# Moving the layer-1 ada products into the pool projection, and the dense chunk of a mixed step ahead of its transposes

## Chip, cores and metric

The kernel runs on one core of one Trainium2 chip. The metric is the device time of one execution in microseconds (us); lower is better. The profile is one execution taken by the hardware profiler on that core. Engines are PE (TensorE), DVE (VectorE), ACT (ScalarE), POOL (GpSimd) and SP (SyncE, which here only issues DMAs). DMAs are issued by SP, ACT and POOL in the order of their programs.

## What is computed

Two layers of a streaming encoder over 544 rows (512 prompt rows and 32 sample rows), model width 2048, all weights float32. Layer 0 is attention (8 heads of differential attention, 8 heads of latent attention), layer 1 is a pooling mixer. Both are modulated by a conditioning vector.

```python
cond = silu(c)
for i in range(2):
    mod = cond @ w_ada[i] + b_ada[i]
    shift, scale, gate = split(mod, 3)
    h = rmsnorm(x, g_norm[i]) * (1 + scale) + shift
    if i == 0:
        z = h @ w_in_att                       # q, k, v, latents, gate
        o = concat(diff_attention(...), latent_attention(...)) * silu(gate)
        y = o @ w_out_att
    else:
        u, g = split(h @ w_in_pool, 2)
        d = trailing_mean(u_ext, window 2/4/8/16) - u
        y = ((d @ w_grp) * scale_pool * silu(g)) @ w_out_pool
    x = x + gate * y
return rmsnorm(x, g_final), caches
```

The modulation `mod` is a product of a vector with a 2048 x 12288 matrix. Its last 16 column tiles are the gate of layer 1. They are first used at the very end, when layer 1's output is added to x.

## The kernel before

Activations lie transposed: features on the 128 partitions, the 544 rows along the free axis. A weight tile is 128 output features by 2048 inputs (1 MB). A dense product splits weights and activations into a high and a low part and adds three products (hi·hi, hi·lo, lo·hi); so one weight tile is 16 k-steps of 6 matmuls, 96 matmuls of 272 columns, into one of two accumulators of two PSUM banks. `split` (DVE, L1562 and L1563) makes the two parts of a whole tile from `w_raw`; the buffer of the parts has two slots, so the split of tile g waits until tile g-2 is multiplied.

The stages, in order, with the times of the profile:

- to 1014 us: modulation, input projection, latent attention.
- 1014 to 1217 us, the differential attention, L1041 on. It is a hand-written order of 39 mixed steps w. In a step PE makes the scores of unit w (`d_scores`), now and then the transposes of a head's values, the products of a finished head with its values (`d_values`), the transposes of unit w-3 (`d_turn`), and a chunk of 2 or 3 of the 8 k-steps of a dense half tile (`latent_half`, the latent heads' half of the output projection; three steps make one half tile). DVE makes the row maximum of unit w, ACT the two exponentials (L1381), DVE the normalised scores (L1862), ACT and DVE the two parts of the transposed scores (L1403 and L1883). ACT may write the exponentials of unit w only when unit w-3 is transposed (`df_tr`), as three buffers rotate. `evict_half` (ACT, L1353) empties the dense half tile from PSUM after every third step, and PE's next half tile waits for it; the result goes over POOL (an addition to x) and `store_half` to memory.
- 1217 to 1282 us: the end of the attention, and the loads of the next stage.
- 1282 to 1440 us, here called the O2 loop: the differential heads' half of the output projection, 16 half tiles (g = 81 to 96) of 48 matmuls. For each, ACT evicts with the gate (L1467), ACT makes the upper part of a later tile's weights (`half_hi`, L1339), DVE adds to x (`update`, L1923) and makes the lower part (`half_lo`, L1819), ACT squares, POOL adds the squares. Beside each half tile DVE makes one ada product: `ada_tile` (L1600) multiplies a 1 MB tile `w_adr` with the two conditioning rows `cond_b` and sums, 128 x 2048 twice, then copies two numbers into `mod`. The tiles of `w_adr` (two buffers) are loaded by ACT (`load_ada`, L1235), which waits for the product that frees the buffer.
- 1440 to 1477 us: the norm of layer 1 (`row_scale`, `affine1`, `make_h1`).
- 1477 to 1852 us, the pool projection (PIN): 16 turns t of two tiles, the u tile A(t) and the gate tile B(t). DVE in a turn: split of B(t), wait for ACT's copy of u, windows and differences, split of A(t+1), wait for the store of the differences. SP loads the tiles of `w_in_pool` into the two slots of `w_raw` as the splits free them.
- to the end: group maps, output projection, final norm.

The SP program around the change issues, in order: `sel_row`, `cond_b` (2 MB), two `w_adr` tiles (1 MB each), two half tiles of `w_out` (0.5 MB each), x back from memory.

## Time and profile before

| what | value |
|---|---|
| median of 3 runs | 2124.44 us (2120.06 to 2126.26) |
| profiled execution, its own time | 2125.24 us |
| its span in the trace | 2123.5 us |
| PE busy | 1876.0 us (88%) |
| DVE busy | 1272.3 us (60%) |
| ACT busy | 454.6 us (21%) |
| POOL busy | 198.6 us (9%) |
| mean DMA rate | 149 GB/s |
| chain that ended last, PE's share | 70% |
| chain that ended last, DVE's share | 14% (L1600: 4%) |

The shares are of the whole span. The digits of PE in 40 slices are 9 nearly everywhere from slice 7 on; they fall to 8 and 7 between slices 19 and 27 (1000 to 1470 us), which is where the change works. The clock granted to PE falls there too, to 7 and 8 tenths.

### The profile page before, as it was taken

Reading aid. Unit: us, or ns where it says so; the run is one execution under the profiler, and the core shown is the slowest. Engines: PE = TensorE matmul, PEld = TensorE weight load, DVE = VectorE, ACT = ScalarE, POOL = GpSimd, SP = SyncE. Lnnn points to the kernel's source line nnn. Section 1 sums busy time; section 2 is a strip of 40 time slices with the busy share of each in tenths; the row PEclk is TensorE's granted clock in tenths of the full one; section 3 lists DMA queues with packets and bytes.
Section 4 is the critical chain, followed back from the end, with each engine's and each line's share of the span. In section 5 each row is a group of like instructions: output and inputs, shape, how many; then the busy total and the mean of one; then the engine's idle time right before and its main releaser. Section 6 shows DMA issues by size and latency. Waiting matters only on the chain.

```text
span 2123.5 us, 32736 instructions
## 1 busy us (share of the span) xinstructions
PE 1876.0 (88%) x13182; PEld 1724.6 (81%) x13182; DVE 1272.3 (60%) x1598; ACT 454.6 (21%) x959; POOL 198.6 (9%) x117
## 2 busy tenths in 40 slices
PE   4539999999999969998888887776999999999995
PEld 0109999999999957767777767765999999999995
DVE  4898766767867644551556547788333444483444
ACT  1241000000011013231555433223111111131111
POOL 3760000000600000000000011110000000001110
PEclk8779999999999999997889988886999999999997
DMA  9565554556545331214333264441333233462222
GB/s 392 207 239 187 199 204 184 201 196 236 209 184 207 131 114 54 67 67 119 102 115 117 89 235 165 168 157 51 109 115 108 100 107 123 150 203 97 81 79 84
DMA packets 86104, 316.04 MB, mean 149 GB/s; under 512 B 12184, under 2 KB 20552, under 8 KB 60448
## 3 DMA queue, kind: packets, MB, share of 16 engines
q1 hardware_dynamic: 62192, 223.02, 29.2%
q10 hardware_dynamic: 23216, 91.16, 12.1%
q0 software_dynamic: 640, 1.10, 0.1%
q8 instruction: 36, 0.59, 0.1%
q14 instruction: 20, 0.16, 0.0%
HBM read 282.56 MB, written 32.69 MB: 148 GB/s over the span
## 4 chain that ended last, share of the span: by engine, by line
PE 70%; DVE 14%; ACT 5%; DMA 3%; issue 3%; POOL 2%; ACTq 1%; SPq 0%; DVEq 0%; POOLq 0%
PE banks L712 70%; DVE banks L1600 4%; POOL ssq L670 2%; DMA w_more<-in_w_ada_pe 1%; ACT pxd L1381 1%; DMA w_raw<-in_w_out 1%; DVE std L1835 1%; ACT w_hi L1339 1%; DVE h_lo L394 1%; DMA d_raw<-pool_d_scratch 1%; ACT stage L1467 1%; DVE rstd L1542 1%; DVE x L2029 0%; DVE w_lo L1563 0%; DMA sgd<-gate_scratch 0%
## 5 line engine op out<-in xcount | busy, mean ns | idle before, releaser
L712 PE MATMUL banks<-h_hi,w_hi 128*128 128x272 f32 x3968 | 836.7, 297 | 76.6 <-DVE w_lo L1819 33.3
L712 PE MATMUL banks<-h_lo,w_hi 128*128 128x272 f32 x3712 | 783.2, 293 | 0.0
L712 PE MATMUL banks<-h_hi,w_lo 128*128 128x272 f32 x3456 | 728.3, 293 | 0.0
L712 PEld LDWEIGHTS banks<-h_hi,w_hi 128*128 128x128 f32 x3968 | 639.9, 195 | 89.8 <-issue 66.2
L712 PEld LDWEIGHTS banks<-h_lo,w_hi 128*128 128x128 f32 x3712 | 601.2, 194 | 0.0
L712 PEld LDWEIGHTS banks<-h_hi,w_lo 128*128 128x128 f32 x3456 | 552.7, 193 | 0.0
L1600 DVE CUSTOM_DVE_ANT_0 banks<-w_adr,cond_b 128x2048 f32<-128x2048 f32 x160 | 402.3, 2514 | 18.6 <-DMA w_adr<-in_w_ada_dve 11.4
L1562 DVE CAST w_hi<-w_raw 128x2048 fp32r<-128x2048 f32 x101 | 125.6, 1244 | 215.4 <-PE banks L712 210.9
L1563 DVE TENSOR_TENSOR w_lo<-w_raw,w_hi 128x2048 fp32r<-128x2048 f32 x101 | 249.2, 2467 | 3.5
L1245 ACT ACTIVATE stage<-banks 128x544 f32<-128x544 f32 x48 | 30.2, 629 | 515.3 <-PE banks L712 515.3
L695 POOL TENSOR_TENSOR ssq<-ssq,stage 128x544 f32<-128x544 f32 x32 | 49.7, 1552 | 790.5 <-ACT stage L1168 790.5
L1923 DVE TENSOR_TENSOR x<-x,stage 128x544 f32 (+1 forms) x32 | 23.2, 725 | 138.0 <-ACT stage L1467 138.0
L1965 DVE TENSOR_TENSOR w<-u_ext 128x573 f32<-128x573 f32 x16 | 12.1, 756 | 138.8 <-ACT u_ext L1490 138.8
L1467 ACT ACTIVATE stage<-banks,mod 128x272 f32<-128x272 f32 (+2 forms) x96 | 32.6, 410 | 250.3 <-PE banks L712 165.7
L712 PE MATMUL banks<-w_more,cond_t 128*2 128x512 f32 x80 | 43.4, 700 | 36.9 <-DMA w_more<-in_w_ada_pe 23.2
L712 PEld LDWEIGHTS banks<-w_more,cond_t 128*2 128x2 f32 x80 | 7.0, 93 | 72.0 <-issue 44.3
L712 PE MATMUL banks<-w_raw,cond_t 128*2 128x512 f32 x48 | 29.1, 764 | 34.5 <-DMA w_raw<-in_w_ada_pe 34.5
L712 PEld LDWEIGHTS banks<-w_raw,cond_t 128*2 128x2 f32 x48 | 4.3, 98 | 57.6 <-DMA w_raw<-in_w_ada_pe 32.0
L712 PE MATMUL banks<-cq,wq 128*128 128x272 f32 x128 | 34.3, 425 | 14.2 <-DVE cq L1698 9.0
L1381 ACT ACTIVATE pxd<-banks,std 128x128 f32<-128x128 f32 (+3 forms) x64 | 33.2, 524 | 60.6 <-DVE std L1836 38.5
L701 POOL TENSOR_TENSOR cos_t<-cos_t,kpe 128x544 f32<-128x544 f32 x8 | 10.8, 1353 | 372.2 <-ACT act_tmp L1357 372.2
L712 PEld LDWEIGHTS banks<-cq,wq 128*128 128x128 f32 x128 | 25.7, 206 | 21.5 <-issue 16.0
(296 smaller groups left out, 1735.8 us busy)
## 6 DMA issues: line engine op xcount, KB each, us to landing
w_adr<-in_w_ada_dve ACTq DMA_DIRECT2D x60, 1024.0 KB, 4.9
w_raw<-in_w_z SPq DMA_DIRECT2D x32, 1024.0 KB, 6.2
w_raw<-in_w_pin SPq DMA_DIRECT2D x32, 1024.0 KB, 4.8
w_adr<-in_w_ada_dve SPq DMA_DIRECT2D x20, 1024.0 KB, 4.9
w_raw<-in_w_gate SPq DMA_DIRECT2D x16, 1024.0 KB, 6.6
w_raw<-in_w_out SPq DMA_DIRECT2D x32, 512.0 KB, 3.8
w_raw<-in_w_pout SPq DMA_DIRECT2D x16, 1024.0 KB, 4.9
w_more<-in_w_ada_pe SPq DMA_DIRECT2D x10, 1024.0 KB, 7.3
```

The costliest lines, as they stand in the source:

```text
L394: ins = eng.scalar_tensor_tensor(out=h_lo[:, k, r], in0=x[:, k, r], scalar=mod[:, c, k:k + 1], in1=h_hi[:, k, r].bitcast(F32), op0=ALU.add ...
L670: pool.tensor_tensor(ssq[:], ssq[:], (stage[:, 0], rstd[:])[k % 2], ALU.add).then_inc(sq_added, 1)
L695: pool.tensor_tensor(ssq[:], ssq[:], stage[:, s], ALU.add).then_inc(sq_added, 1)
L712: return pe.matmul(out, lhsT, rhs, start=start, stop=stop)
L1245: act.activation(rows(stage[:, s]), acc[slot], func).then_inc(acc_free[slot], 1)
L1339: act.activation(half_slots(g)[0], w_raw[:, g % 2, 0:D // 2], ACT.Copy).then_inc(w_upper, 1)
L1381: ins = act.activation(pxd[:, w % 3, e, 0:n], PS[:, 2 * (w % 2) + e, 0:n], ACT.Exp, bias=std[:, w, 2 + e:3 + e], scale=DIFF_SCALE, accum_o ...
L1467: ins = act.activation(stage[:, s, r], PS[:, 2 * slot + bank, cols], ACT.Identity, scale=mod[:, c, bass.ds(2 * t + (gate_tile + s), 1)])
L1562: vchain(dve, dve.tensor_copy(w_hi[:, slot], w_raw[:, slot]))
L1563: dve.tensor_tensor(w_lo[:, slot], w_raw[:, slot], w_hi[:, slot].bitcast(F32), ALU.subtract).then_inc(split_ready, 1)
L1600: ins = dve.tensor_tensor_reduce(ada_junk, w_adr[:, slot], cond_b[:, c, :], 1.0, 0.0, ALU.mult, ALU.add, ada_acc[:, c:c + 1])
L1923: dve.tensor_tensor(at(x, t2 + k), at(x, t2 + k), stage[:, slot], ALU.add).then_inc(x_new, 1)
```

## The change

- The 16 ada products of layer 1's gate leave the O2 loop. They are made in the first 8 turns of the pool projection, two in each: one after the split of B(t), one after the split of A(t+1).
- There they have one buffer, `w_adr[:, 1]`, as the first one's place is used by `u_ext`, `w2` and `w4`; a filler `under_ada` moves `d_st` and `fix` behind `w_adr` and `cond_b`. Their 16 loads are issued by SP, in turn t behind those of A(t) and B(t), each waiting until the product before it is done. The two loads ahead of the O2 loop and ACT's loads in it are gone.
- The Silu of `cond_b` on ACT moves from before the O2 loop to behind `affine1`, and DVE's wait for it to before the first turn of the pool projection.
- In a mixed step PE makes the dense chunk after the values' transposes and before `d_values` and `d_turn`; before, it came last.
- ACT's `evict_half` moves from the end of every third step to the start of the step after it, `store_half` to the end of the step with w % 3 == 1. The small ACT instruction that told POOL of the eviction (`x1_ev`) is gone; POOL waits for `acc_free`.

```diff
+        sb("under_ada", [P, 6466], scope=pin_stack)
...
@@ SP
-            for s in range(2):
-                load_ada(s, w_ada_dve[ADA_P0 + ADA_P1 + s])
...
-            with sp.Fori(0, KT) as t:
+            with sp.Fori(0, KT // 2) as t:
                 for s in range(2):
                     load_w(tile_of(wp2, s, t), (G_PIN + s) % 2, 2 * t + G_PIN - G_KPE + s)
+                for s in range(2):
+                    sp.wait_ge(adr_used, 2 * t + (ADA_P0 + ADA_P1 + s))
+                    sp.dma_start(w_adr[:, 1], tile_of(wd2, s, t + (ADA_P0 + ADA_P1) // 2)).then_inc(adr_in[s], 16)
+            with sp.Fori(KT // 2, KT) as t:
+                for s in range(2):
+                    load_w(tile_of(wp2, s, t), (G_PIN + s) % 2, 2 * t + G_PIN - G_KPE + s)
+            sp.wait_ge(adr_used, ADA_P0 + ADA_P1 + KT)
@@ POOL
-                pool.wait_ge(x1_ev, n + 1)
+                pool.wait_ge(acc_free[(G_OUT + n) % 2], turn_of(G_OUT + n) + 1)
@@ PE, a mixed step
+                if w < 3 * IN_STEPS:
+                    latent_half(w // 3, chunk_of[w % 3])
                 for h in range(HEADS):
                     if w == d_last(h) + DLAG + 1:
                         d_values(h)
                 if DLAG <= w < D_UNITS + DLAG:
                     d_turn(w - DLAG)
-                if w < 3 * IN_STEPS:
-                    latent_half(w // 3, chunk_of[w % 3])
@@ ACT, evict_half
-                act.wait_ge(acc_free[g % 2], turn_of(g) + 1)
-                act.activation(act_tmp[0:1, 0:1], act_tmp[0:1, 0:1], ACT.Copy).then_inc(x1_ev, 1)
@@ ACT, a mixed step
-            for w in range(D_UNITS + DLAG + 2):
+            for w in range(D_UNITS + DLAG + 1):
+                if w % 3 == 0 and w:
+                    evict_half(w // 3 - 1)
...
-                if w < 3 * IN_STEPS and w % 3 == 2:
-                    if w // 3:
-                        store_half(w // 3 - 1)
-                    evict_half(w // 3)
+                if w % 3 == 1 and w > 3:
+                    store_half(w // 3 - 1)
...
-            act.wait_ge(condb_in, 32)
-            act.activation(cond_b[:], cond_b[:], ACT.Silu).then_inc(condb_ready, 1)
...
-                gated(t, G_O2, 1, 2 * KT, ADA_P0 + ADA_P1, True)
+                gated(t, G_O2, 1, 2 * KT, halves=True)
...
             affine1()
+            act.wait_ge(condb_in, 32)
+            act.activation(cond_b[:], cond_b[:], ACT.Silu).then_inc(condb_ready, 1)
@@ DVE, O2 loop
-            dve.wait_ge(condb_ready, 2)
...
-                    ada_tile(ADA_P0 + ADA_P1 + s, 2 * t, t)
                     update(G_O2 + s, 2 * t, t, 1, s, s)
                     half_lo(G_O2 + s + 2, 2 * t, t)
...
-                ada_tile(ADA_P0 + ADA_P1 + k, 0, 0)
@@ DVE, pool projection
+            dve.wait_ge(condb_ready, 2)
             for grp, w in enumerate(WIN):
                 with dve.Fori(4 * grp, 4 * grp + 4) as t:
...
                     split(G_PIN + 1, dve_t2, t)
+                    if grp < 2:
+                        ada_tile(ADA_P0 + ADA_P1, dve_t2, t, 1)
                     dve.wait_ge(acc_free[us], t + turn_of(G_PIN + 2))
...
                     split(G_PIN + 2, dve_t2, t)
+                    if grp < 2:
+                        ada_tile(ADA_P0 + ADA_P1 + 1, dve_t2, t, 1)
                     dve.wait_ge(d_stored, 16 * t + 16)
+                if grp == 1:
+                    add_bias(ADA_PE + ADA_P0 + ADA_P1, ADA_T)
```

## Rows read from the trace of the kernel before

**Rows 1.** Stretch, us, busy of PE, PEld, DVE, ACT, POOL; PE's clock, DMA share, GB/s.

```profile
1014.00:1213.00 199.00, 168.78 (x1228) 147.56 (x1227) 115.86 (x260) 108.49 (x297) 16.22 (x12) 0.89 0.34 108
...
1282.00:1440.00 158.00, 112.03 (x716) 108.35 (x715) 126.58 (x117) 41.70 (x81) 26.43 (x17) 0.83 0.47 162
...
1477.00:1574.00 97.00, 96.75 (x772) 96.76 (x773) 36.80 (x49) 16.13 (x26) 0.00 (x0) 1.00 0.34 121
```

**Rows 2.** The chain that ended last: start us, us, what, count.

```profile
1242.18 14.67 DMA w_raw<-in_w_out
...
1438.32 2.19 PE banks L712 x4
...
1477.25 373.11 PE banks L712 x2976
```

**Rows 3.** PE's waits, 1213 to 1480 us: waited for, total us, times, longest.

```profile
PE banks L712 <- DVE w_lo L1819: 33.3, 14, 4.6
```

**Rows 4.** Timeline of DVE, one half tile and the end of the O2 loop.

```profile
1291.36 3.43 DVE L1600 CUSTOM_DVE_ANT_0 banks<-w_adr,cond_b 128x2048 f32<-128x2048 f32 x1
...
1299.23 0.73 DVE L1923 TENSOR_TENSOR x<-x,stage 128x544 f32 x1 [1.67 <-ACT stage L1467]
1300.05 1.22 DVE L1819 TENSOR_TENSOR w_lo<-w_raw,w_hi 128x1024 fp32r<-128x1024 f32 x1
1301.19 3.44 DVE L1600 CUSTOM_DVE_ANT_0 banks<-w_adr,cond_b 128x2048 f32<-128x2048 f32 x1
...
1435.44 0.72 DVE L1923 TENSOR_TENSOR x<-x,stage 128x544 f32<-128x544 f32 x1
```

**Rows 5.** Timeline of PE between half tiles 82 and 83.

```profile
1286.60 0.41 PE L712 MATMUL banks<-h_hi,w_lo 128*128 128x272 f32 x2
1291.58 0.81 PE L712 MATMUL banks<-h_hi,w_hi 128*128 128x272 f32 x2 [4.57 <-DVE w_lo L1819]
```

**Rows 6.** DMA issues of three moments: engine, count, KB, us to landing.

```profile
cond_b<-in_cB SPq DMA_DIRECT2D x1, 2048.0 KB, 9.8
...
w_adr<-in_w_ada_dve SPq DMA_DIRECT2D x1, 1024.0 KB, 4.8
w_raw<-in_w_z SPq DMA_DIRECT2D x1, 1024.0 KB, 6.6
...
w_raw<-in_w_out SPq DMA_DIRECT2D x2, 512.0 KB, 6.3
```

**Rows 7.** Timeline of ACT and DVE: the Silu, and the entry of the pool projection.

```profile
1278.78 3.62 ACT L1456 ACTIVATE cond_b<-cond_b 128x4096 f32<-128x4096 f32 x1
...
1472.01 1.28 ACT L1486 ACT_TABLE_LOAD   x1
...
1473.64 1.23 DVE L1562 CAST w_hi<-w_raw 128x2048 fp32r<-128x2048 f32 x1 [0.32 <-DVE h_lo L1581]
1474.90 2.29 DVE L1563 TENSOR_TENSOR w_lo<-w_raw,w_hi 128x2048 fp32r<-128x2048 f32 x1
```

**Rows 8.** Timeline of DVE: an ada product beside the input projection, POOL idle.

```profile
184.61 2.29 DVE L1600 CUSTOM_DVE_ANT_0 banks<-w_adr,cond_b 128x2048 f32<-128x2048 f32 x1
...
189.50 0.17 DVE L1606 COPY mod<-ada_acc 128x2 f32 x1
```

**Rows 9.** PE's waits in the mixed steps, 1014 to 1213 us.

```profile
PE banks L1012 <- DVE pxd L1862: 11.8, 4, 3.0
PE banks L1009 <- ACT od L1411: 5.3, 3, 1.8
```

**Rows 10.** Timeline of mixed steps 5 to 8: PE and ACT.

```profile
1044.33 1.00 ACT L1353 ACTIVATE rstd<-banks,mod 128x272 f32<-128x272 f32 x3
...
1042.97 1.11 PE L1012 MATMUL banks<-id_t,pxd 128*128 128x128 f32 x4 [2.96 <-DVE pxd L1862]
1045.48 0.79 PE L712 MATMUL banks<-h_hi,w_hi 128*128 128x272 f32 x2 [1.39 <-ACT rstd L1353]
...
1052.70 0.37 ACT L1381 ACTIVATE pxd<-banks,std 128x128 f32<-128x128 f32 x1 [2.63 <-PE banks L1012]
```

More of the change, by code:

```diff
@@ L361, in program @@
         x_new = sem("x_new")
-        w_upper = sem("w_upper"); x1_ev = sem("x1_ev"); x1_added = sem("x1_added")
+        w_upper = sem("w_upper"); x1_added = sem("x1_added")
         x1_in = [sem(f"x1_in{s}") for s in range(2)]
@@ L1593, in make_h1, with ada_tile @@
                 dve.wait_ge(h_ready, 2 * KT + 2)
-            def ada_tile(a, t2, t):
+            def ada_tile(a, t2, t, buf=None):
                 slot = a % 2
@@ L1599, in ada_tile @@
                 for c in range(2):
-                    ins = dve.tensor_tensor_reduce(ada_junk, w_adr[:, slot], cond_b[:, c, :], 1.0, 0.0, ALU.mult, ALU.add,
+                    ins = dve.tensor_tensor_reduce(ada_junk, w_adr[:, slot if buf is None else buf], cond_b[:, c, :], 1.0, 0.0, ALU.mult, ALU.add,
                                                    ada_acc[:, c:c + 1])
@@ L1926, in _ @@
             half_lo(G_O2 + 1)
-            dve.wait_ge(condb_ready, 2)
             dve.wait_ge(x_in, 32)
             with dve.Fori(0, KT // 2 - 2) as t:
-                dv.loop(t, 4)
                 for s in range(2):
-                    ada_tile(ADA_P0 + ADA_P1 + s, 2 * t, t)
                     update(G_O2 + s, 2 * t, t, 1, s, s)
                     half_lo(G_O2 + s + 2, 2 * t, t)
-            dv.end(KT // 2 - 2)
             dve.wait_ge(x_rest_in, 16)
             for k in range(KT - 4, KT):
-                ada_tile(ADA_P0 + ADA_P1 + k, 0, 0)
                 update(G_O2 + k, 0, 0, 1, k, k % 2)
@@ L1943, in _ @@
                     split(G_PIN)
-            add_bias(ADA_PE + ADA_P0 + ADA_P1, ADA_T)
             dve.memset(lam_in[:, 0, 0:1], 0.0).then_inc(pad_free, 1)
@@ L1955, in _ @@
                     t0 = t - 4 * grp
-                    dv.loop(t0, 2 + grp + 1 + 1 + 1)
+                    dv.loop(t0, 2 + grp + 1 + 1 + 1 + (4 if grp < 2 else 0))
                     dve_t2 = 2 * t
                     split(G_PIN + 1, dve_t2, t)
+                    if grp < 2:
+                        ada_tile(ADA_P0 + ADA_P1, dve_t2, t, 1)
                     dve.wait_ge(acc_free[us], t + turn_of(G_PIN + 2))
```

## Prediction

> **What bounds the kernel now.** I read the busy time by stretch first, then the chain that ended last, then PE's waits and the timelines of the two loops. PE is the bound of the whole, but not of every stage [rows 1]: in the pool projection it is busy 96.75 of 97 us at full clock (2.4 GHz) while DVE works 36.8 us; in the O2 loop it is busy 112 of 158 us at a mean clock of 0.83, and DVE 127 of 158. PE there waits 33.3 us in 14 waits for the lower part of the weights [rows 3]. One half tile shows why: DVE's round from one ada product to the next is 1301.19 - 1291.36 = 9.83 us, of which `update` and `half_lo` are 0.73 and 1.22 and the product the most [rows 4]. So the O2 loop is bound by DVE, through the products, which nobody needs there. The reader should see one engine short in one stage and long in the next.
>
> A full tile costs PE 373.11 us / 31 = 12.04 us at full clock: 2976 matmuls are 31 tiles of 96 [rows 2]. A half tile is then 6.02 us, a turn of the pool projection 24.07 us.
>
> **Part 1: the end of the attention.** SP no longer issues two 1 MB loads between `cond_b` and the first half tile of `w_out`. That tile's landing is on the chain with 14.67 us [rows 2]. A second 1 MB transfer issued 0.4 us behind a first lands 6.6 + 0.4 - 4.8 = 2.2 us after it; 2 MB alone take 9.8 [rows 6]. The wait falls to between 9.8 (the row of 2 MB, as if half a megabyte cost nothing more) and 14.67 - 4.4 = 10.3; with what was issued in between I take 5.0 us gained. All that follows up to half tile 82 moves with it. The Silu of `cond_b` (1.28 us table, 3.62 us [rows 7]) stood on ACT between half tile 82's weights and the first eviction; PE was multiplying 82 meanwhile, so it costs nothing by itself once the products are gone.
>
> **Part 2: the O2 loop.** Half tile 82 ended at 1286.9 [rows 5]; now 1281.9. Half tile 83 needs its weights: SP issues them behind the last part of x, after `store_half(15)`, which also moves by 5; they land 6.3 us after issue [rows 6], near 1280.4, and the two parts (about 1.0 on ACT, 1.2 on DVE) are there at 1282.7, 0.8 us late. What is late next in the loop? Per half tile DVE now has 0.73 + 1.22 us, ACT the eviction and `half_hi` (about 1 us each) and a square of 0.7, and the chain from the end of g to the weights of g+2 is about 3.5 us, 4.7 if POOL holds DVE up once; PE works 6.02 us on g+1 meanwhile. So PE is the bound, and its clock stays at the upper level as in the pool projection [rows 1]. Fourteen half tiles: 1282.7 + 84.3 = 1367.0. From the last matmul to the row sums: eviction and semaphore 1.2 us, then as now from `update` (1435.44) to the row sums (1438.32) 2.9 us [rows 2, 4]: 1371.1. The gain up to that point is 1438.3 - 1371.1 = 67.2 us, part 1's 5.0 included. Bounds: 8 us less if a half tile takes 6.6 us, nothing more.
>
> **Part 3: the entry of the pool projection.** The norm is unchanged, 33 us on DVE. Then DVE waits for the Silu before the split of B(0). ACT ends `affine1` at 1472.0, where its next table load starts [rows 7]; table 1.28 and Silu 3.62 end at 1476.95, and DVE began the split at 1473.64 [rows 7]. PE waits for this split (it ended at 1477.2, where PE's long piece begins [rows 2]). Cost 3.3 us, all on the path.
>
> **Part 4: the turns with products.** A product with its copy takes 189.67 - 184.61 = 5.06 us beside a busy PE and an idle POOL [rows 8]; in the O2 loop the first half took 3.43 instead of 2.29 [rows 4] with POOL at work, and POOL is idle in the pool projection [rows 1]. Two in a turn are 10.1 us on a DVE busy 36.8 in four turns, 9.2 in each: 19.3 of 24.07 us. By busy time they are hidden. By order they are not, because one buffer and SP's order tie the loads to the products. Per turn, in order, the end of one releasing the next: the split of A(t+1), 3.5 us [rows 7]; the product behind it, 5.06; only then SP issues the next `w_adr` tile, 4.8 + 0.1 us to landing less 0.2 as the semaphore comes before the copy, 4.7 [rows 6]; the product of that tile, 5.06; only then SP issues the other `w_adr` tile and, behind it on the same queue, A(t+2), which lands 0.4 + 6.6 us later less 0.2, 6.85 [rows 6]; then its split. The sum is 3.5 + 5.06 + 4.7 + 5.06 + 6.85 + 0.2 of handovers = 25.4 us against PE's 24.07. The loop is PE's no longer, by 1.3 us a turn. In the first turn, counted from the end of B(0)'s split: product 5.06, A(1) lands at 11.9, is split at 15.5, and PE, done with B(0) at 12.03, waits 3.4 us. The eighth such split ends at 15.5 + 7 x 25.4 = 193.3; PE would have been there at 12.03 + 7 x 24.07 = 180.5. Cost 12.8 us, with part 3 16.1. Queued behind DVE's waits are the windows and splits; behind SP's wait for `adr_used` the tiles of `w_in_pool`, which is the whole cost. ACT waits for `d_ready` before the gate's Silu, and PE needs that accumulator only a tile later. From turn 8 on everything is as before.
>
> Bounds: if the loop hides under PE, 3.3 + 3.4 = 6.7 us; if A lands only when all three queued megabytes are in (2 MB alone take 9.8 [rows 6]; 2.4 more a turn), 15.5 + 2.4 + 7 x 27.8 - 180.5 + 3.3 = 35.3. I take 16, as the row with two megabytes in a queue is the nearest.
>
> The Trainium skill, DMA: Bandwidth & Descriptors, Rules for kernel authors, advises to issue a DMA early, compute, and wait for it late. The new loop does the reverse for half of its loads. The same page, Bandwidth, gives 6.15 us for 1 MB where this trace has 4.8 [rows 6]; an estimate with the page's figure adds 1.35 us to each of the two landings in a turn and would make the turn 28.1 us. The trace's duration is the one I use.
>
> **Part 5: the mixed steps.** PE waits for the normalised scores 11.8 us in four waits and for the eviction of `od` 5.3 us [rows 9]; a chunk put in front (18 matmuls, 2.3 us) covers part of these. But the order speaks against it twice. Step 6 shows the first: PE waited 2.96 us for the scores, transposed, then 1.39 us for the eviction on ACT, 1044.33 + 1.0 [rows 10]. The chunk needs that eviction, so in front of the transposes it waits for both; ACT's place for it is the same as before, as nothing stood between the end of step 5 and the start of step 6. The second: ACT's exponentials of unit w wait until w-3 is transposed. This bound already in step 7, 2.63 us idle [rows 10]; now the transposes come one chunk, 2.3 us, later in every step. ACT and DVE pass work to one another, so part of this reaches the next step. Followed through steps 3 to 15 with the durations of the timeline, the chunk of step 6 comes 1.5 us later and that of step 15 2.8: 1.3 us per nine steps, 5.4 for four such groups. The last `store_half` comes one step earlier, so SP reaches the load of `sgd` sooner, about 1.3 us. I take +4 us. Bounds: the two waits covered whole, -17; one chunk lost in each of the 12 handovers of a half tile, +28; for the range I use -12 and +12. The dropped ACT instructions and POOL's other semaphore (0.2 us, 16 times) lie beside PE's work; nothing.
>
> **The sum**, against the profiled execution's own 2125.24 us: -67.2 + 3.3 + 12.8 + 4.0 = -47.1, so 2078.1. That execution stands 0.8 us above the median of the three runs, which changes nothing; I give 2078.
>
> **The rivals.**
> - The loop with products hides (A lands sooner, the handovers are shorter): the cost of parts 3 and 4 is 6.7 instead of 16.1, 2069. For it: the margin is 1.3 us in 25.4. Against: the row of the landing is direct. Chance 0.15.
> - The mixed steps gain: the chunk covers the waits of rows 9, -12 instead of +4, 2062. For it: 17 us of waits stand right behind the scores. Against: rows 10. Chance 0.15.
> - Late landing: A(t+1) lands with the third tile of its queue; 35.3 instead of 16.1, 2097. For it: 9.8 us for 2 MB. Beside this stands a rule of the Trainium skill, DMA: Bandwidth & Descriptors, Queues, rings and completion order: completion is not first in, first out for one issuing engine. Chance 0.12.
> - Something else bounds the O2 loop: PE's half tile becomes 7.2 us, because POOL's additions stretch DVE's `half_lo` or the 0.5 MB loads come late: 14 x 1.2 = 17 us less gained, 2095. Against: 3.5 us of work in a 6.02 us window. Chance 0.08.
> - Slower: the single buffer of `w_adr`. If both landings of the chain in part 4 take 3.8 us more, near 8.6 and 10.6 (2 MB took 9.8), the turn is 33 us: 7 x 9 + 10.5 = 73 against 63 gained, 2135. It decides from 32 us a turn. Nothing but the first loads behind `cond_b` comes near that. Chance 0.04.
> - The change doesn't do what it says: a wait left in place keeps ACT's eviction in the O2 loop behind something else, and the loop stays at 9.8 us a tile while the products cost as well: about 2132. I find no such wait. Chance 0.01.
> - My forecast: 0.45.
>
> **The numbers.** The likeliest case gives 2078. The range that holds 8 in 10 takes the two faster rivals and the late landing in: 2060 to 2099. 0.3% (6.4 us) is about what a measurement tells from no change; faster than that are all cases but the last two, 0.94, slower 0.05, same 0.01.
>
> **What would show it.** PE's waits for `half_lo` in the O2 loop near zero, the loop 84 to 88 us for 14 half tiles, clock near 1.0. DVE's wait for `cond_b` before the first turn. In the turns with products: pieces of PE separated by 1 to 2 us, waits for DVE's w_lo L1563 and behind them w_raw, period 25.4; DVE waiting for w_adr about 1 us twice a turn or less; SP's waits for the product. In the mixed steps: no wait for pxd, a longer one for the eviction (up to 7 us in step 6), ACT waiting for PE's transposes far more than now. I am wrong if the period is under 24.2 or over 27, if a half tile is over 6.4 us, or if the mixed steps move by more than 8 us.

## The result: 0.5% faster, where 2.2% was forecast

The changed kernel takes 2112.28 us (median of 6 runs, 2108.93 to 2112.97), the kernel before 2123.07 beside it (6 runs). The ratio is 0.9947, with a 95% interval of 0.9933 to 0.996. It is faster by about 11 us. The forecast was 47 us less, and the range ended at 2060 and 2099: the time lies above it.

The profiled execution of the changed kernel took 2112.39 us, with a span of 2110.6 (before 2125.24 and 2123.5), so the two traces differ by 12.9 us and can be compared stage by stage. Line numbers are up by 4 to 6: TensorE's products are L718 (were L712), the transposes L1018, the evictions of the mixed steps L1359, the exponentials L1387, DVE's product L1604, the split L1566 and L1567, `half_lo` L1823.

The chain that ended last, of the changed kernel (start us, us, what, count), to be read beside [rows 2]; the row at 1404.36 is the row sums of layer 1's norm:

```profile
1273.96 11.37 DMA w_raw<-in_w_out
...
1315.95 84.46 PE banks L718 x672
...
1404.36 2.19 PE banks L718 x4
...
1438.06 1.28 ACT L1484
1439.35 3.63 ACT cond_b L1484
1443.35 1.24 DVE w_hi L1566
...
1452.59 6.72 DMA w_raw<-in_w_pin
...
1467.80 4.87 DMA w_adr<-in_w_ada_dve
...
1478.47 6.69 DMA w_raw<-in_w_pin
```

The reader sees the O2 loop as one piece of PE (672 matmuls, 14 half tiles), then the Silu in front of B(0)'s split, then landings of `w_raw` in every turn, where before one piece of 373.11 us stood. The loop itself went as forecast. But it starts late: `w_out` is asked for at 1273.96, and at 1242.18 before. These 31.8 us lie in the mixed steps, ahead of all the rest. The same stretch of both traces shows it (first before, then after; stretch, us, busy of PE, PEld, DVE, ACT, POOL; PE's clock, DMA share, GB/s):

```profile
1014.00:1243.00 229.00, 197.50 (x1420) 170.19 (x1418) 131.72 (x278) 120.65 (x320) 19.25 (x14) 0.91 0.36 115
```

```profile
1014.00:1243.00 229.00, 185.22 (x1237) 162.49 (x1238) 113.04 (x261) 106.01 (x284) 16.19 (x12) 0.80 0.28 94
```

PE does fewer matmuls in the same time, is idle for 12 us more, and its mean clock is 0.80 instead of 0.91. The waits of that stretch after the change (waited for, us in total, times, longest), first ACT's, then PE's; before, the exponentials waited 21.7 us in 7 for the transposes, and PE 4.6 and 2.8 for the evictions:

```profile
ACT pxd L1387 <- PE banks L1018: 74.7, 15, 10.4
ACT pxd L1387 <- DVE std L1840: 28.8, 17, 2.7
```

```profile
PE banks L718 <- ACT rstd L1359: 17.8, 4, 7.0
PE banks L718 <- ACT kpe L1359: 17.0, 5, 7.0
```

PE's wait for `pxd` [rows 9] is gone, as forecast. In its place PE waits 34.8 us for evictions, where it was 7.4.

Cutting the two profiles at the same events gives the whole difference:

| stretch, from which event to which | before | after | change | forecast |
|---|---|---|---|---|
| start to the issue of `w_out` (mixed steps) | 1242.18 | 1273.96 | +31.8 | +4.0 |
| landing of `w_out` | 14.67 | 11.37 | -3.3 | -5.0 |
| landing to the row sums (O2 loop) | 181.5 | 119.0 | -62.4 | -62.2 |
| row sums to the end of B(0)'s split (Silu) | 38.9 | 42.5 | +3.6 | +3.3 |
| from there to the eighth split of an A (before: PE's own time for it, 180.5, worked out in the prediction) | 180.5 | 197.9 | +17.4 | +12.8 |

The sum is -12.9, which is the difference of the spans; what follows the last row takes the same time in both within 0.2 us. One term of five is wrong by 28 us, another by 4.6, and the landing by 1.7.

### The profile page after: what moved, and what is told of

It reads as the page before. It is cut to its first block, busy times and chain, and to the rows that moved or that the text cites. A ratio compares the mean times of both kernels' runs of the same rounds, so it can differ in the third digit from the quotient of the medians.

```text
span 2110.6 us, 32711 instructions
## 1 busy us (share of the span) xinstructions
PE 1874.6 (89%) x13182; PEld 1722.4 (82%) x13182; DVE 1253.6 (59%) x1598; ACT 411.3 (19%) x912; POOL 198.4 (9%) x117
## 4 chain that ended last, share of the span: by engine, by line
PE 65%; DVE 13%; DMA 8%; ACT 6%; issue 5%; POOL 2%; SPq 1%; DVEq 0%; ACTq 0%; POOLq 0%
PE banks L718 65%; DVE banks L1604 3%; DMA w_raw<-in_w_pin 3%; POOL ssq L676 2%; DMA w_adr<-in_w_ada_dve 2%; DMA w_more<-in_w_ada_pe 1%; ACT pxd L1387 1%; DMA d_raw<-pool_d_scratch 1%; DMA w_raw<-in_w_out 1%; DVE w_hi L1566 1%; DVE std L1839 1%; DVE h_lo L395 1%; DVE w_hi L1823 1%; DVE rstd L1546 1%; DVE x L2034 0%
## 5 line engine op out<-in xcount | busy, mean ns | idle before, releaser
L718 PE MATMUL banks<-h_hi,w_hi 128*128 128x272 f32 x3968 | 832.7, 295 | 86.6 <-DVE w_lo L1567 29.6
L718 PE MATMUL banks<-h_lo,w_hi 128*128 128x272 f32 x3712 | 778.1, 292 | 0.0
L718 PE MATMUL banks<-h_hi,w_lo 128*128 128x272 f32 x3456 | 721.0, 290 | 0.0
L718 PEld LDWEIGHTS banks<-h_hi,w_hi 128*128 128x128 f32 x3968 | 634.6, 194 | 98.9 <-issue 72.6
L718 PEld LDWEIGHTS banks<-h_lo,w_hi 128*128 128x128 f32 x3712 | 596.3, 193 | 0.0
L718 PEld LDWEIGHTS banks<-h_hi,w_lo 128*128 128x128 f32 x3456 | 545.7, 191 | 0.0
L1604 DVE CUSTOM_DVE_ANT_0 banks<-w_adr,cond_b 128x2048 f32<-128x2048 f32 x160 | 386.2, 2414 | 19.2 <-DMA w_adr<-in_w_ada_dve 16.0
L1566 DVE CAST w_hi<-w_raw 128x2048 fp32r<-128x2048 f32 x101 | 125.6, 1244 | 220.1 <-PE banks L718 169.4
L1567 DVE TENSOR_TENSOR w_lo<-w_raw,w_hi 128x2048 fp32r<-128x2048 f32 x101 | 249.2, 2467 | 3.5
L718 PE MATMUL banks<-w_more,cond_t 128*2 128x512 f32 x80 | 43.7, 704 | 39.0 <-DMA w_more<-in_w_ada_pe 22.8
L718 PEld LDWEIGHTS banks<-w_more,cond_t 128*2 128x2 f32 x80 | 7.0, 94 | 74.3 <-issue 47.1
L1887 DVE TENSOR_TENSOR ptd_lo<-banks,ptd_hi 128x128 fp32r<-128x128 f32 (+3 forms) x32 | 15.7, 492 | 81.4 <-ACT ptd_hi L1409 81.4
L718 PE MATMUL banks<-w_raw,cond_t 128*2 128x512 f32 x48 | 29.0, 760 | 32.6 <-DMA w_raw<-in_w_ada_pe 32.6
L1387 ACT ACTIVATE pxd<-banks,std 128x128 f32<-128x128 f32 (+3 forms) x64 | 33.2, 524 | 103.5 <-PE banks L1018 74.7
L718 PEld LDWEIGHTS banks<-w_raw,cond_t 128*2 128x2 f32 x48 | 4.3, 98 | 55.6 <-DMA w_raw<-in_w_ada_pe 30.2
L718 PE MATMUL banks<-cq,wq 128*128 128x272 f32 x128 | 34.3, 425 | 14.3 <-DVE cq L1702 9.0
```

What stands on the lines that cost most here:

```text
L718: return pe.matmul(out, lhsT, rhs, start=start, stop=stop)
L1387: ins = act.activation(pxd[:, w % 3, e, 0:n], PS[:, 2 * (w % 2) + e, 0:n], ACT.Exp, bias=std[:, w, 2 + e:3 + e], scale=DIFF_SCALE, accum_o ...
L1566: vchain(dve, dve.tensor_copy(w_hi[:, slot], w_raw[:, slot]))
L1567: dve.tensor_tensor(w_lo[:, slot], w_raw[:, slot], w_hi[:, slot].bitcast(F32), ALU.subtract).then_inc(split_ready, 1)
L1604: ins = dve.tensor_tensor_reduce(ada_junk, w_adr[:, slot if buf is None else buf], cond_b[:, c, :], 1.0, 0.0, ALU.mult, ALU.add, ada_acc[: ...
```

## Experiments: is it the mixed steps, and which part of them?

Every ratio below is against the kernel before, measured beside the run. The runs were made in four groups, in which its medians were 2126.40, 2127.52, 2124.97 and 2126.65 us; beside the changed kernel it was 2123.07. So differences between medians of different groups are uncertain by some 4 us.

**One or both parts undone.** The first run keeps the move of the products and takes the steps back; the others add the steps, or one of their two edits, to the kernel before.

```diff
                 if DLAG <= w < D_UNITS + DLAG:
                     d_turn(w - DLAG)
+                if w < 3 * IN_STEPS:
+                    latent_half(w // 3, chunk_of[w % 3])
```

(Cut to TensorE's order of before; in the first run `x1_ev` and the evictions and stores at the end of the third step come back too.)

> The changed kernel with its mixed steps put back as they were (TensorE's dense chunk last, evictions at the end of the third step of a half tile, the x1_ev operation); the products stay moved. Theory A, the loss sits in the mixed steps and is worth what their stretch shows (58.3 us per nine steps against some 50 to 51.5 before, four and a half turns of nine, about 31 us): 2112 - 31 = 2081 us, so 0.98 of before. Rival B, the mixed steps cost the 4 us that was forecast and the rest of the gain went elsewhere in the program: 2112 - 4 = 2108 us. Between 2095 and 2100 neither is right alone.

Measured: 2080.28 us, ratio 0.979 (0.9764 to 0.9816). The steps cost 32.0 us, theory A. Rival B is out. With them taken back, the kernel is near the forecast, in part by luck: without the 4 us that the forecast gave to the steps it would have been 2074, and the 6 us above that are the 4.6 and 1.7 us by which part 4 and the landing were off.

The next three start from the kernel before: both edits, the order alone, the evictions alone. The edit on ScalarE, cut to its main lines (the old places of the eviction and the store go, and with them `x1_ev`), is

```diff
-            for w in range(D_UNITS + DLAG + 2):
+            for w in range(D_UNITS + DLAG + 1):
+                if w % 3 == 0 and w:
+                    evict_half(w // 3 - 1)
...
+                if w % 3 == 1 and w > 3:
+                    store_half(w // 3 - 1)
```

> The kernel before with the mixed steps of the changed one (dense chunk ahead of the transposes, evictions at the start of the next half tile's first step, no x1_ev operation) and nothing else. Theory A (the steps alone cost about 31 us): 2123 + 31 = 2154 us, ratio 1.015. Rival B (4 us): 2127 us, ratio 1.002. Rival C, the steps are slow only because the products no longer stand elsewhere, which would make the two parts not add up: within 0.3% of before, 2117 to 2129.

Measured: 2157.93 us, ratio 1.0161 (1.0132 to 1.019), 31.5 us above before: the two parts of the change add up, and the steps' loss does not depend on the products.

> The kernel before with one edit: TensorE does the dense chunk ahead of the transposes; ScalarE's evictions stay at the end of the third step. Theory A1, the order on TensorE is all of the loss: 2150 to 2158 us, the same as with both edits. Rival A2, the loss comes from the evictions that stand behind the next turn's start: about 2123, within 0.3% of before. Rival A3, each needs the other: with evictions at the end of the third step and the chunk early, the next half tile's chunks find their banks free earlier and the time falls below before, to 2105 to 2117 us.

Measured: 2157.91 us, ratio 1.0156 (1.013 to 1.0183). TensorE's order is all of the loss (A1).

> The kernel before with the other edit alone: ScalarE evicts a half tile at the start of the next half tile's first step, stores in its second, and GpSimd waits for the eviction itself; TensorE's chunk stays last. Theory A1 (TensorE's order is the loss): 2120 to 2126 us, no change. Rival A2 (the place of the evictions is the loss): 2145 to 2158 us. Rival A3 (they hold only together): 2120 to 2126 too, so this run parts A2 from the others and the run with the chunk alone parts A1 from A3.

Measured: 2125.29 us, ratio 0.9997 (0.9984 to 1.001). The evictions' place and the dropped operation are worth nothing, as the prediction said.

**The mechanism.** Two places of every nine steps hold the long waits; waits of 2.95 and 2.5 us at two others complete the 74.7 us. The first is step 12, where the sample values stand. Timeline of the changed kernel, PE and then ACT (start us, us, engine, line, operation, count, in brackets the idle time before it):

```profile
1081.70 1.91 PE L718 MATMUL banks<-ptds,vcs 128*128 128x32 f32 x8
...
1086.52 0.82 PE L718 MATMUL banks<-h_hi,w_hi 128*128 128x272 f32 x2
...
1090.60 0.27 PE L1018 MATMUL banks<-id_t,pxd 128*128 128x128 f32 x1
```

```profile
1079.55 1.02 ACT L1359 ACTIVATE rstd<-banks,mod 128x272 f32<-128x272 f32 x3
1090.97 0.69 ACT L1387 ACTIVATE pxd<-banks,std 128x512 f32<-128x512 f32 x1 [10.39 <-PE banks L1018]
```

ACT has evicted by 1080.6, and its next exponentials need a buffer that one transpose of 0.27 us sets free. In front of that transpose PE now has scores, sample values and the chunk, 10.5 us of work. The clock was at its lower level, 1.2 GHz, all through: eight sample products took 1.91 us, scores and sample values together 6.5 us, and the chunk 4.1 us. In the kernel before, the clock was at its upper level when the scores and sample values came (3.9 us), and this step's chunk stood behind the transpose. But that chunk ran at the lower level there too, and took 4.0 us, from 1079.64 to 1083.60:

```profile
1076.88 1.08 PE L712 MATMUL banks<-ptds,vcs 128*128 128x32 f32 x8
...
1079.64 0.75 PE L712 MATMUL banks<-h_hi,w_hi 128*128 128x272 f32 x2
...
1083.60 0.50 PE L712 MATMUL banks<-kd_hi,qd_hi 64*128 64x512 f32 x2
```

So of the 6.6 us by which the work in front of the transpose grew, 4.1 are the chunk at its own price and 2.5 the lower clock on the rest.

The second place is step 15, three steps on:

```profile
1105.79 0.79 PE L718 MATMUL banks<-h_hi,w_hi 128*128 128x272 f32 x2 [6.97 <-ACT kpe L1359]
...
1110.01 1.01 PE L1018 MATMUL banks<-id_t,pxd 128*128 128x128 f32 x4
```

```profile
1104.64 1.01 ACT L1359 ACTIVATE kpe<-banks,mod 128x272 f32<-128x272 f32 x3
1111.12 0.47 ACT L1387 ACTIVATE pxd<-banks,std 128x256 f32<-128x256 f32 x1 [5.47 <-PE banks L1018]
```

PE waits 6.97 us for an eviction (1.39 before, at 1097.13). ACT then waits for the transposes behind the chunk. The chunk takes 4.2 us (mean clock 0.51 from 1105 to 1111); in the kernel before it took 3.8 (mean clock 0.60 from 1097.13 to 1100.92). One waits for the other in turn, where before PE's chunk ran beside ACT's exponentials.

**Waiting or slower work.** ACT's sample exponentials mark the period. Between the first and the last of them lie 27 steps, with the same matmuls in every kernel (columns as in the result's stretches; first before, then after):

```profile
1058.34:1207.70 149.36, 126.41 (x929) 110.58 (x929) 84.58 (x197) 79.04 (x221) 12.14 (x9) 0.91 0.34 109
```

```profile
1062.73:1236.37 173.64, 141.22 (x928) 123.73 (x927) 82.65 (x197) 76.90 (x212) 12.13 (x9) 0.79 0.28 93
```

The stretch grew by 24.3 us. PE is idle 9.5 us more (32.4 against 23.0), and busy 14.8 us more with the same work, at a mean clock of 0.79 instead of 0.91. This is an account and no experiment: at the upper level part of the 14.8 us could have turned into waits. The runs that follow are best read in the same way:

| run | start of the first marker | the 27 steps | PE busy in them | PE idle |
|---|---|---|---|---|
| before | 1058.3 | 149.4 | 126.4 | 23.0 |
| changed kernel | 1062.7 | 173.6 | 141.2 | 32.4 |
| every first chunk behind | 1061.4 | 158.1 | 132.3 | 25.9 |
| first chunk of 3, 12, 21, 30 behind | 1058.1 | 172.1 | 136.8 | 35.3 |
| first chunk of 6, 15, 24, 33 behind | 1061.8 | 171.7 | 138.9 | 32.8 |
| four buffers | 1055.1 | 153.1 | 129.1 | 24.0 |
| wait filled | 1056.7 | 172.5 | 149.1, filler included | 23.4 |

**Which chunk.** Three runs move the chunk back behind the transposes in some steps: in 0, 3, 6, ... (below); with `w % 9 == 3`, which has the steps with sample values 12, 21 and 30 (and step 3, which has none); and with `w % 9 == 6`, those behind the wait of 6.97 us.

```diff
-                if w < 3 * IN_STEPS:
+                if w < 3 * IN_STEPS and w % 3:
                     latent_half(w // 3, chunk_of[w % 3])
...
+                if w < 3 * IN_STEPS and w % 3 == 0:
+                    latent_half(w // 3, chunk_of[0])
```

> The changed kernel, but the first dense chunk of each half tile (steps 0, 3, 6, ...) goes back behind the step's values and transposes; the other two stay ahead of them. In the trace of the changed kernel every long wait of TensorE (6.97 us, in one first chunk of three) and every long wait of an exponential (10.39 us behind the sample values, 5.47 us) lies at a first chunk. Theory C, the loss comes from these: the chunk that itself waits for an eviction holds back the transposes that ScalarE needs before the next one. Then most of the 31 us comes back: 2082 to 2092 us. Rival D, each chunk ahead costs its own 2.4 to 4 us in front of a transpose, whichever it is: only a third comes back, 2098 to 2106 us.

Measured: 2088.53 us, ratio 0.9819 (0.9786 to 0.9853). some 24 of the 32 us come back with one chunk of three: theory C. (The four times spread from 2083.37 to 2093.17, and the trace is of the longest.)

> The changed kernel with the chunk back behind the transposes in the steps with sample values alone (3, 12, 21, 30). Theory K, these steps start it: sample values (5 us at the low clock) and the chunk (4.3 us) both stand before one short transpose, the exponentials wait 10.39 us, and everything on ScalarE, the eviction for which TensorE waits 6.97 us later too, is late by that. Then this alone brings back 15 to 24 us: 2088 to 2097 us. Rival L, the two places are separate costs: 4 to 10 us come back, 2102 to 2108 us.

Measured: 2108.76 us, ratio 0.9928 (0.99 to 0.9955): 3.5 us back by the medians, which is not clear of the noise (the changed kernel's interval, 0.9933 to 0.996, overlaps), a little less than rival L had, and far from theory K. ACT's longest wait falls from 10.4 to 6.1 us, but the sum stays:

```profile
ACT pxd L1389 <- PE banks L1018: 74.0, 18, 6.1
```

> The changed kernel with the chunk back behind the transposes in steps 6, 15, 24 and 33 alone, where TensorE waits 6.97 us for the eviction and then does the chunk at the low clock while the exponentials wait 5.47 us. Theory K (the steps with sample values start it): the transposes no longer wait for the eviction here, which brings back the 5.47 us of the exponentials in four places at most, less what moves to the next wait: 5 to 14 us, 2098 to 2107 us, less than the other run. Theory M, this is the place that starts it: 15 us or more, 2088 to 2097 us.

Measured: 2102.81 us, ratio 0.9893 (0.9867 to 0.9919); 9.5 us back by the medians, 4.2 by the spans of the traces. The number is in theory K's range, but K wanted less here than in the run before, and that one took K away; M's 15 us are not reached. K was argued from the two timelines above, and the table does not bear it: by the traces, of what the run with 3, 12, 21 and 30 gained, 4.6 us lie ahead of the first marker, where step 3 has no sample values, and only 1.6 in the 27 steps.

Neither place carries the loss alone: 3.5 and 9.5 are 13 us together (1.6 and 2.0 in the 27 steps), and all first chunks at once give 24 (15.5). Two explanations are left. The run with every first chunk also moves those of steps 0, 9, 18, 27 and 36, which neither of the two others does; at step 9 PE waits 1.38 us for the eviction, and the exponentials at 1068.06 wait 2.95 us for the transposes behind it. Or a wait that goes at one place comes back at the next, as long as another first chunk still stands in front. No run moves the third group alone, or any two of the three, so this stays open.

**The buffers.** The exponentials of step w overwrite what step w-3 left, so they need the transposes that PE does in step w itself. A fourth buffer moves that one step back.

```diff
-        pxd = sb("pxd", [P, 3, 2, NP], scope=dif)
+        pxd = sb("pxd", [P, 4, 2, NP], scope=dif)
...
-                        if w >= 3 and w % 9 != 2:
-                            act.wait_ge(df_tr, w - 2)
+                        if w >= 4 and w % 9 != 3:
+                            act.wait_ge(df_tr, w - 3)
```

> The changed kernel with four buffers for the exponentials instead of three, so that the exponentials of a step wait for the transposes of one step earlier (the tile vrs moves elsewhere to make room; all the work is kept). Theory E, the chain that costs the time runs from an eviction on ScalarE to TensorE's chunk, from there to the transposes behind it, and from these to the next exponentials: the 74.7 us of exponentials waiting for transposes fall below 30 and at least 20 us come back, 2080 to 2092 us. Rival F, TensorE waits for the evictions whatever the exponentials do, and the exponentials only wait because TensorE is late: no more than 6 us come back, 2106 to 2112 us.

Measured: 2086.9 us, ratio 0.9822 (0.9795 to 0.9848): 25 us come back, theory E. (The trace is of the fastest of the four, 2080.28 us.) The waits of ACT and PE in the same stretch are

```profile
ACT pxd L1387 <- DVE std L1840: 45.8, 32, 2.7
```

```profile
PE banks L718 <- ACT rstd L1359: 14.4, 4, 6.2
PE banks L718 <- ACT kpe L1359: 13.3, 5, 6.1
```

The exponentials wait for no transpose any more. PE's waits for evictions fall only from 34.8 to 27.7 us. They seem to have a cause of their own: ACT evicts when it has done a whole step, and the chunk now asks for that early. That they are the part of the loss that stays is argued.

**The clock.** In steps 6, 15, 24 and 33, 36 additional matmuls each fill PE's wait; their result is overwritten.

```diff
+                pe.wait_ge(df_exp, w)
+                for k in range(count):
+                    small(PS[:, 2 * ((w + 1) % 2), 0:240], w_hi[:, 0, 0:P], h_hi[:, HEADS, 0:240], True, True)
```

> The changed kernel with 36 additional matmuls of 240 columns in steps 6, 15, 24 and 33, between the scores and the first dense chunk, where TensorE waits 6.97 us for the eviction; their result is overwritten by the next scores. They wait for the exponentials of the step before (1101.04 in the trace, where the wait runs from 1098.82 to 1105.79) and last 3.5 to 4 us at the full clock, so they take no time from the chunk. They part the wait from the clock: the chunk and transposes behind the wait take 5.2 us now and 3.2 at the full clock. Theory G, the clock's fall behind that wait costs about 2 us in each of four places and brings more waits: 2098 to 2106 us. Rival H, the low clock there is covered by other waits, or the filler runs at the low clock itself and delays the chunk: 2110 to 2122 us.

Measured: 2107.76 us, ratio 0.9924 (0.9896 to 0.9953), 4.5 us back by the medians. That lies between the two theories (G ended at 2106, H began at 2110), and the interval overlaps the changed kernel's. Step 15 of that run; the first row is the 36 additional matmuls and the first two of the chunk:

```profile
1095.18 6.18 PE L718 MATMUL banks<-h_hi,w_hi 128*128 128x240 f32 x38 [2.27 <-ACT pxd L1395]
1101.19 0.41 PE L718 MATMUL banks<-h_lo,w_hi 128*128 128x272 f32 x2
...
1103.20 0.60 PE L1018 MATMUL banks<-id_t,pxd 128*128 128x128 f32 x4
1103.72 0.33 PE L718 MATMUL banks<-kd_hi,qd_hi 64*128 64x128 f32 x2
```

```profile
1098.73 1.01 ACT L1367 ACTIVATE kpe<-banks,mod 128x272 f32<-128x272 f32 x3
...
1103.89 0.47 ACT L1395 ACTIVATE pxd<-banks,std 128x256 f32<-128x256 f32 x1 [4.15 <-PE banks L1018]
```

Chunk and transposes run at the upper level (1.00 from 1101 to 1106), the four transposes in 0.60 us instead of 1.01, and the exponentials wait 4.15 us here instead of 5.47. All in all they still wait 73.4 us for transposes. But the filler was not free: it ran largely at the lower level itself (mean clock 0.71 from 1095.18 to 1100.98), took 5.7 us where 3.5 to 4 had been expected, and ended 1.1 us after the eviction (1099.74) for which the chunk had waited; in the last of the four places it was 3.5 us. So the run shows that the clock behind these waits is worth something, not how much: 4.5 us is what was left after the filler's own cost. By the traces the first marker comes 6.0 us earlier, and the 27 steps are only 1.1 us shorter. The low clock at the sample values was not filled at all.

## Experiments: the turns with products and the Silu

These start from the first run (steps as before, 2080.28 us).

```diff
...
+            with sp.Fori(0, KT // 2 - 1) as t:
+                load_w(tile_of(wp2, 1, t), (G_PIN + 1) % 2, 2 * t + G_PIN - G_KPE + 1)
+                load_w(tile_of(wp2, 0, t + 1), G_PIN % 2, 2 * t + G_PIN - G_KPE + 2)
+                sp.wait_ge(adr_used, 2 * t + (ADA_P0 + ADA_P1 + 1))
...
+                sp.wait_ge(adr_used, 2 * t + (ADA_P0 + ADA_P1 + 2))
```

> The changed kernel with its mixed steps as before and another order of SyncE's loads in the eight turns with products: the second and the next first tile of the input projection are issued ahead of the two waits for products, so each load of w_raw goes out when its buffer is free and not when a product is done. Theory I, the 21 us that these turns cost are this order: a load of w_raw stands behind a wait for a product, and DVE's products alone fit in the turn of 24.07 us, as the eight turns without them have it. The turns with products fall from 25.94 to about 24.1 us and the first by some 3 us: 2062 to 2067 us. Rival J, the products themselves fill DVE or the channels past 24 us: at most 5 us come back, 2075 to 2080 us.

Measured: 2085.7 us, ratio 0.9811 (0.978 to 0.9841): no gain, and 5.4 us above the same kernel without the new order, above rival J's range too. J's reason was not shown either: DVE was not full. A turn takes 27.2 us (1484.85 to 1512.06) instead of 25.97. SP's and DVE's timeline, SP's first:

```profile
1483.98 0.33 SPq L636 DMA_DIRECT2D w_adr<-in_w_ada_dve  x1
1484.85 0.92 SPq L470 DMA_DIRECT2D w_raw<-in_w_pin  x2
```

```profile
1491.89 1.23 DVE L1577 CAST w_hi<-w_raw 128x2048 fp32r<-128x2048 f32 x1 [7.76 <-DMA w_raw<-in_w_pin]
```

Both `w_raw` loads still stood behind the wait for the second product of the turn before. My order had only moved that wait. The next run issues each load in the order in which DVE lets its buffer go:

```diff
...
+            with sp.Fori(0, KT // 2 - 1) as t:
+                load_w(tile_of(wp2, 1, t + 1), (G_PIN + 1) % 2, 2 * t + G_PIN - G_KPE + 3)
+                sp.wait_ge(adr_used, 2 * t + (ADA_P0 + ADA_P1 + 1))
+                sp.dma_start(w_adr[:, 1], tile_of(wd2, 1, t + (ADA_P0 + ADA_P1) // 2)).then_inc(adr_in[1], 16)
+                load_w(tile_of(wp2, 0, t + 2), G_PIN % 2, 2 * t + G_PIN - G_KPE + 4)
+                sp.wait_ge(adr_used, 2 * t + (ADA_P0 + ADA_P1 + 2))
+                sp.dma_start(w_adr[:, 1], tile_of(wd2, 0, t + ((ADA_P0 + ADA_P1) // 2 + 1))).then_inc(adr_in[0], 16)
```

> The changed kernel with mixed steps as before and a third order of SyncE's loads in the turns with products: each load is issued in the order in which DVE lets go of its buffer (second w_raw tile after its split, w_adr after its product, first w_raw tile, w_adr). In the run with the loads ahead the order was wrong: both w_raw loads still left together behind a product (1484.85, right after w_adr at 1483.98) and DVE then stood 7.76 us for the first. Theory I', the cost of the turns with products is this order: no w_raw load stands behind a product, a turn is 24.1 us, and about 14 us of the turns' cost come back: 2063 to 2068 us. Rival J, DVE's products fill the turn by themselves: 2076 to 2082 us, as without the new order.

Measured: 2063.34 us, ratio 0.9709 (0.9688 to 0.9729), 16.9 us below the same kernel without the new order, theory I'. The chain has the input projection as one piece again, and PE is busy all through the turns with products, with DVE at 160.8 of 205 us:

```profile
1414.74 205.36 PE banks L727 x1619
```

```profile
1415.00:1620.00 205.00, 205.00 (x1620) 205.00 (x1621) 160.82 (x194) 12.73 (x40) 0.00 (x0) 0.99 0.55 188
```

So the products hide fully under PE, and SP's order was the cause of the 17.4 us of the result's table, within 0.5 us. The Trainium skill, DMA: Bandwidth & Descriptors, Rules for kernel authors, asks for early issue and a late wait; this pair (2080.28 and 2063.34 us) bears it out for loads that one engine issues in order.

```diff
             root(1)
-            affine1()
             act.wait_ge(condb_in, 32)
             act.activation(cond_b[:], cond_b[:], ACT.Silu).then_inc(condb_ready, 1)
+            affine1()
```

> The kernel of the loads in turn, with the Silu of cond_b on ScalarE ahead of affine1 instead of behind it, where ScalarE waits for the row sums' root and the fold. If the 3.6 us that Silu stands in the chain (1439.35, 3.63 us, of the changed kernel) is a matter of its place, 3 to 5 us below the kernel with the loads in turn; if ScalarE's work behind it only waits elsewhere or the table is loaded twice more, within 1 us of it.

Measured: 2057.66 us, ratio 0.9686 (0.9668 to 0.9703), 5.7 us less by the medians. By the traces, from the row sums to the end of B(0)'s split, it is 3.7. ACT's row shows where the Silu went, beside DVE's reciprocal:

```profile
1377.70 3.62 ACT L1494 ACTIVATE cond_b<-cond_b 128x4096 f32<-128x4096 f32 x1
```

The last two add the fourth buffer (the diff above), and then TensorE's order of the changed kernel with the evictions left where they were.

> The last one with four buffers for the exponentials and the chunk last, as before. In the steps before the change, exponentials wait 21.7 us for transposes in seven places and 38.5 us for DVE's maxima. If the seven waits are on the path: 5 to 12 us below the kernel with three buffers; if the next thing (DVE's maxima, the transposes waiting for DVE's pxd) takes their place: within 3 us of it.

Measured: 2057.71 us, ratio 0.9687 (0.9666 to 0.9708): nothing. With the chunk last, the fourth buffer frees exponentials that then wait for something else: no wait for transposes is left, but 52.7 us for DVE's maxima (39.6 with three buffers). PE's wait for `pxd` is 11.8 us as before.

> The same with the dense chunk ahead of the transposes. With three buffers that order costs 31 us. If the chain through the three buffers is all that speaks against it, the order costs nothing here or gains: from 8 us below to 2 us above the kernel with four buffers and the chunk last. If the evictions behind the chunk are a cost of their own, 5 us or more above it.

Measured: 2065.8 us, ratio 0.9721 (0.9703 to 0.974), 8.1 us above the last one. So even with a fourth buffer the early chunk is the worse order here. Beside it stand PE's longer waits for evictions (27.8 us in nine, against 9.0 in seven) and a mean clock of 0.87 instead of 0.91 over the 27 steps; no run parts the two.

The best kernel of the study is the one with the products moved, the steps as before, the loads in turn and the Silu early: 2057.66 us, 3.1% below the kernel before.

## Why the prediction was wrong, step by step

**What bounds the kernel, and parts 1 and 2: right.** The O2 loop is PE's, 84.46 us for 14 half tiles against 84.3 forecast, mean clock 1.00 from 1316 to 1400, and one wait of 0.8 us for the half tile's lower part, also as forecast. The landing fell by 3.3 instead of 5.0 us: 11.37 us, which is outside the bounds for it (9.8 to 10.3). (By [rows 5] half tile 82 ended at 1287.0 and not at 1286.9, which changes nothing.)

**Part 3, the Silu: right**, 3.6 for 3.3.

**Part 4: right in its mechanism, short in size.** The first A was split 16.1 us after B(0) (forecast 15.5), the period was 25.97 (1644.73 - 1462.95 over seven) instead of 25.4. The term that was short is SP's. The chain of the seventh such turn:

```profile
1607.32 0.04 SPq L632
...
1607.45 0.33 SPq L632
...
1608.31 6.70 DMA w_raw<-in_w_pin
```

From the product's end (1607.30) to the `w_raw` transfer SP takes 1.0 us, where the sum had 0.4, and the landing is 6.7 to 7.2 instead of 6.6. The period grew by 0.57 us and the first turn by 0.6, which makes 17.4 instead of 12.8 in all. By the Trainium skill's 6.15 us for 1 MB (DMA: Bandwidth & Descriptors, Bandwidth, a table of transfers issued from GpSimd) the estimate was 28.1 us a turn; a `w_adr` tile issued from SyncE lands here in 4.87 us and the turn takes 25.97, and the measurement decides. The rival in which the loop hides needed another order of the loads, not shorter handovers.

**Part 5, the mixed steps: wrong, and it decides the case.** The failed step is the sentence "Followed through steps 3 to 15 with the durations of the timeline, the chunk of step 6 comes 1.5 us later and that of step 15 2.8". Step 6's chunk came 2.0 us later (1047.48, against 1045.48 in [rows 10]); step 15's 8.7 (1105.79 against 1097.13). Between them lies step 12 with its 10.39 us. The signs were right: both causes that the prediction names are in the trace, the waits are those that the prediction named as its signs (6.97 us for the eviction in step 6, "up to 7 us"; ACT waiting for transposes 74.7 us instead of 21.7), and theory E's run shows that the three buffers carry most of the loss. What failed is the price. Two things were wrong in the walk.

- The price of the work in front of a transpose. The only price that the prediction gives for a chunk is 2.3 us, that of the upper clock level. In step 12 scores, sample values and chunk took 10.5 us, where the rows of before give 6.3 with such a chunk (3.9 from 1075.64 to 1079.56, and 2.4). Of the 4.2 us between them, 1.6 could be read in the trace of before, where this chunk takes 4.0 us; 2.5 are the lower clock on scores and sample values, which only the new order shows. These 4.2 us are most of what step 15 was later than forecast (5.9), if they passed on whole, which is argued.
- The walk stopped after one group of nine steps and multiplied. The 27 steps between the markers, 149.36 and 173.64 us, are 49.8 and 57.9 us per nine. That is 8.1 each instead of 1.3. The first group was already 4.4 us late at its marker.

The range failed for another reason. The prediction had its own upper bound at +28, one chunk lost at each handover, and used +12 "for the range" with no row for it. With +28 alone the forecast would have come to 2102, two thirds of the way to what was measured. Even that bound took a chunk at 2.3 us; in the two bad places it takes 4.1 and 4.2. The case "mixed steps lose much" was not among the rivals at all, though rows 10 showed both of its parts; the rivals had only the gain.

**What was named as the sign of an error** was met: "if the mixed steps move by more than 8 us". The other two (period, half tile) held.

**What stays open.** How much of the 32 us the clock would give back. Over 27 steps PE spends 14.8 of the 24.3 additional us on the same work at a lower clock, but the run that filled four waits got back only 4.5, less its filler's cost. Open too is what is left when most of the loss is back. With every first chunk behind, 8.2 us stay, and the trace shows PE waiting for `pxd` (18.5 us in five, 11.8 in four before); with the fourth buffer 6.6 us stay, and it shows PE waiting for evictions. No run separates them further. And which first chunks matter is not settled, as said above.

## What to carry to other kernels

Work that an engine puts in front of a short operation delays whoever waits for that operation, here by 10.5 us at the worst step. Ask first how many buffers lie between the two engines (a fourth gave back 25 us of 32), and look at the step in which most work is queued ahead, not at the mean one. Take the price of a piece of work from the place where it stands in the trace: a chunk of 18 matmuls took 2.4 us in one step and 4.0 in another. Follow a periodic schedule through more than one period before multiplying. A load belongs in the issuing queue at the place where its buffer is let go: two waits in the wrong order cost 17 us here, though every transfer was short enough to hide. And a bound that the rows give belongs in the range whole, though here even that would have ended short.

## What was not expected of the hardware

In the changed kernel the granted clock was 1.00 until 1076.6, 1.2 us past the end of a wait of 1.77 us, and 0.50 from 1076.8 to 1090.3. A wait of 0.81 us lies in that stretch, and behind it 10.6 us in which PE never stood, of which this is a part (columns as above):

```profile
1081.00:1090.00 9.00, 9.00 (x41) 8.19 (x38) 2.34 (x7) 0.00 (x0) 1.06 (x1) 0.50 0.20 60
```

These 9 us at half the clock are 4.5 us of work. The kernel before shows that the lower level needs no new wait in front of it. Around the same step its clock was 0.50 from 1073 to 1076, behind a wait of 1.77 us, 1.00 from 1076.5 to 1079.5, and 0.50 once more, though PE had not stood since 1072.7:

```profile
1079.70:1083.00 3.30, 3.30 (x16) 3.30 (x16) 0.29 (x1) 2.96 (x8) 0.00 (x0) 0.50 0.55 159
```

So a wait is no sure sign of the lower level, and busy work no sure sign of the upper one; the granted clock of the stretch has to be read.
